# Two b loops of a matmul step become one: which bank each product of a split-precision matmul goes to next

## What is computed

```
h = modulate(rmsnorm(x, g_norm_mix), sh1, sc1);  proj = h @ w_in
y = concat([rg_lru(...) * gelu(gr), pool_mixer(xp)]) @ w_out;  x = x + gt1 * y
h = modulate(rmsnorm(x, g_norm_ffn), sh2, sc2)
x = x + gt2 * ((silu(h @ w_ffn_gate) * (h @ w_ffn_up)) @ w_ffn_down)
...
h = rmsnorm(x, attn_norm_w);  proj = h @ w_in_2            # retention and block attention
x = x + (sigmoid(g_ret) * (o_ret @ w_ret_up) + sigmoid(g_moba) * (o_moba @ w_moba_up)) @ w_out_2
up = causal_dwconv(rmsnorm(x) @ w_ffn_up_2);  x = x + (silu(a) * b) @ w_ffn_down_2
return rmsnorm(x, final_norm_w)
```

## Time and profile before

| | |
|---|---|
| median of three runs | 2616.88 us |
| profiled execution | 2618.59 us |
| its span, first to last instruction | 2616.8 us |
| PE busy | 2538.1 us, 97% |
| PEld busy | 2146.7 us, 82% |
| DVE busy | 1785.6 us, 68% |
| ACT busy | 1180.2 us, 45% |
| mean granted clock of PE | 0.985 |
| DMA | 553.94 MB, 61.3% of 16 engines' span |

### The profile page before, as it was taken

The page is one execution under the profiler, slowest core; times in us unless marked ns, Lnnn a source line. Parts: engine busy times, 40 slices in busy tenths (PEclk is TensorE's granted clock), DMA queues, the critical chain, the costliest instruction groups (busy, mean ns, idle before and its releaser), DMA issues.

```text
span 2616.8 us, 39666 instructions
## 1 busy us (share of the span) xinstructions
PE 2538.1 (97%) x14492; PEld 2146.7 (82%) x14492; DVE 1785.6 (68%) x2301; ACT 1180.2 (45%) x1438; POOL 9.9 (0%) x37
## 2 busy tenths in 40 slices
PE   4999999999999999999999999999999999999997
PEld 0667687888888888888888888888888888888886
DVE  2468698955555555687686565676788668875886
ACT  1345344444444444563444554445544444444443
POOL 1000000000000000000000000000000000000000
PEclk8999998999999999999999999999999999999998
DMA  9968986955555555555554555556555655555553
GB/s 371 403 260 329 382 334 245 357 169 187 191 187 190 186 190 185 164 192 182 178 175 165 166 166 195 183 188 193 177 183 185 202 184 192 190 187 185 185 169 112
DMA packets 156313, 553.94 MB, mean 212 GB/s; under 512 B 16161, under 2 KB 20257, under 8 KB 156209
## 3 DMA queue, kind: packets, MB, share of 16 engines
q1 hardware_dynamic: 155360, 549.85, 61.3%
q0 software_dynamic: 848, 2.69, 0.3%
HBM read 550.38 MB, written 2.10 MB: 211 GB/s over the span
## 4 chain that ended last, share of the span: by engine, by line
PE 89%; DVE 5%; DMA 3%; ACT 1%; issue 1%; SPq 0%; DVEq 0%; ACTq 0%
PE ps L551 54%; PE ps L558 27%; DMA ride<-in_w_ada 3%; PE ps L548 2%; PE pm L579 2%; DVE split L1204 1%; PE ps L555 1%; DVE acc_out L1255 1%; ACT split L872 1%; DVE val L1215 0%; DVE x_t L1327 0%; DVE ssq L1276 0%; PE pm L757 0%; PE pm L662 0%; PE pm L599 0%
## 5 line engine op out<-in xcount | busy, mean ns | idle before, releaser
L1204 DVE TENSOR_TENSOR split<-raw,split 128x1024 fp32r<-128x1024 f32 (+1 forms) x864 | 1031.0, 1203 | 698.9 <-ACT split L872 696.0
L872 ACT ACTIVATE split<-raw 128x1024 fp32r<-128x1024 f32 (+1 forms) x864 | 895.9, 1043 | 1150.6 <-PE ps L558 1095.6
L551 PE MATMUL ps<-h_s,split 128*128 128x512 f32 x3904 | 1242.5, 400 | 13.5 <-DVE split L1204 6.4
L558 PEld LDWEIGHTS ps<-h_s,split 128*128 128x128 f32 x3904 | 738.0, 189 | 175.0
L558 PE MATMUL ps<-h_s,split 128*128 128x256 f32 x3904 | 771.0, 279 | 0.0
L551 PE MATMUL ps<-mid_s,split 128*128 128x512 f32 x2368 | 746.6, 397 | 0.5 <-DVE split L1204 0.4
L551 PEld LDWEIGHTS ps<-h_s,split 128*128 128x128 f32 x3904 | 599.7, 190 | 47.6 <-issue 42.4
L558 PEld LDWEIGHTS ps<-mid_s,split 128*128 128x128 f32 x2368 | 445.5, 188 | 105.5
L558 PE MATMUL ps<-mid_s,split 128*128 128x256 f32 x2368 | 465.7, 278 | 0.0
L551 PEld LDWEIGHTS ps<-mid_s,split 128*128 128x128 f32 x2368 | 361.1, 189 | 7.2 <-issue 5.2
L879 ACT ACTIVATE low<-ps 128x512 f32<-128x512 f32 x232 | 134.4, 579 | 4.4 <-PE ps L558 4.4
(11 more groups left out here) (246 smaller groups left out, 1117.1 us busy)
## 6 DMA issues: line engine op xcount, KB each, us to landing
raw<-in_w_in SPq DMA_DIRECT2D x224, 512.0 KB, 3.3
ride<-in_w_ada SPq DMA_DIRECT2D x64, 1024.0 KB, 8.2
raw<-in_w_ffn_down SPq DMA_DIRECT2D x128, 512.0 KB, 3.5
raw<-in_w_ffn_gate SPq DMA_DIRECT2D x88, 512.0 KB, 3.3
raw<-in_w_ffn_up SPq DMA_DIRECT2D x88, 512.0 KB, 3.5
raw<-in_w_ffn_a SPq DMA_DIRECT2D x88, 512.0 KB, 4.2
raw<-in_w_ffn_b SPq DMA_DIRECT2D x88, 512.0 KB, 4.4
raw<-in_w_out SPq DMA_DIRECT2D x64, 512.0 KB, 5.5
```

The source lines that it names most:

```text
L551: pe.matmul(ps[:, s, b, :], split[:, slot, k, 0, b * P:(b + 1) * P], acts[:, k0 + k, :, :].rearrange("p h t -> p (h t)"), start=start, sto ...
L558: mm = pe.matmul(ps[:, s, b, 0:T], split[:, slot, k, 1, b * P:(b + 1) * P], acts[:, k0 + k, 0, :], start=False, stop=stop)
L872: act.activation(split[:, c, 0:kt, 0, :], raw[:, CHUNKS * s + c, 0:kt, :], ACT.Copy).then_inc(hi_ready, 1)
L1204: dve.tensor_tensor(split[:, c, 0:kt, 1, :], raw[:, CHUNKS * s + c, 0:kt, :], split[:, c, 0:kt, 0, :].bitcast(F32), ALU.subtract).then_inc ...
```

## The change

In each k step the two loops over b are made one. The matmul of 256 columns for a block now stands right behind the one of 512 columns for the same block. The number of matmuls, their operands, waits and increments are the same, and so is the position of the last matmul (b = 1, low weights).

```diff
@@ multiply @@
                 for b in range(2):
                     if tok:
                         pe.matmul(ps[:, s, b, :], acts[:, k0 + k, 0, b * P:(b + 1) * P],
                                   split[:, slot, k, :, :].rearrange("p h n -> p (h n)"), start=start, stop=False)
+                        mm = pe.matmul(ps[:, s, b, 0:SLAB], acts[:, k0 + k, 1, b * P:(b + 1) * P],
+                                       split[:, slot, k, 0, :], start=False, stop=stop)
                     else:
                         pe.matmul(ps[:, s, b, :], split[:, slot, k, 0, b * P:(b + 1) * P],
                                   acts[:, k0 + k, :, :].rearrange("p h t -> p (h t)"), start=start, stop=False)
-                for b in range(2):
-                    if tok:
-                        mm = pe.matmul(ps[:, s, b, 0:SLAB], acts[:, k0 + k, 1, b * P:(b + 1) * P],
-                                       split[:, slot, k, 0, :], start=False, stop=stop)
-                    else:
                         mm = pe.matmul(ps[:, s, b, 0:T], split[:, slot, k, 1, b * P:(b + 1) * P],
                                        acts[:, k0 + k, 0, :], start=False, stop=stop)
             mm.then_inc(chunk_used, 1)
```

## The result

The changed kernel is slower: 2636.67 us is the median of 13 runs, against 2617.17 us for the kernel before (13 runs), a ratio of 1.006 with an interval of 1.0047 to 1.0073. What a median hides is as telling: the runs of before lie within 3 us (2616.65 to 2619.57), those of the changed kernel spread over 19 us (2623.16 to 2642.32). The profiled execution took 2630.16 us. Sixteen more executions of the changed kernel are on record, from 2627.53 to 2642.09 us.

The account below looks back on a forecast made before the run. PE's pace through its k steps was taken to bound the kernel. All terms summed to 0, leaving the profiled 2618.59 us; the runs' median stands 1.7 us lower, so 2616.9 us was forecast, range 2597 to 2651.

Parts of the forecast that it names:

- the price of a same-bank handoff: At the two 512-to-256 handoffs of a step: 5 ns each would give +34 us, 2651 us, the range's upper end.
- The direction that I gave 0.24: The changed kernel comes out slower, because handoffs within one bank cost time; chance 0.24.
- The likeliest case, no change: Whole kernel: no change to within 5.2 us, 2616.9 us with its own range 2611 to 2622; chance 0.56.
- What bounds the kernel, steps and their number: PE's rate through 3392 k steps of 0.696 us sets the time: 2361 us, 90% of the profiled execution.
- Instructions, waits, hand-over points: 0: In each chunk no instruction is added or removed, and waits, increments and hand-over points stay where they were: 0.
- Weight loads: 0 unless they run ahead: Four loads a step, each covered by the matmul ahead: 0; starting two matmuls early would give -54 us, chance 0.08.
- Handoffs: Between a step's matmuls: distance to the next goes with column count, not follower, so 0; rounding allows -54 to +47 us.
- Same bank: 0: A 256 right behind the 512 of its own bank costs nothing extra, judged from the gates' float32 rows: 0.
- The rival on the slower side: Two 512-to-256 handoffs a step cost something within a bank: +34 us at 5 ns, +68 us at 10; chance 0.24.
- Leaving a bank costs: Two of four bank changes a step go: -95 us at 14 ns each, -20 us at 3 ns; chance 0.12.
- The 14 ns a matmul that I asked about: In each 0.696 us step, 0.056 us beyond the columns' time at 2.4 GHz, 14 ns for each of four matmuls.
- A step that differs by more than 1.5 ns proves the forecast wrong: Sign to check in the changed kernel: a step more than 1.5 ns from 0.696 us disproves the forecast, whatever the reason.

Follow-up runs that it names:

- four_wide: Kernel before with every 256-column matmul made 512 wide, so four matmuls of 512 a step: 3318.38 us in one execution.
- six_narrow: Kernel before with every 512-column matmul split into two of 256, each with its own weight load: 2686.95 us in one execution.
- grouped_same_bank: Kernel before with the two 256 of each step in reverse bank order, so two of four handoffs stay in one bank: 2616.71 us, ratio 0.9998.
- starters: Changed kernel with two one-column products put ahead of eleven long stretches: 2620.31 us, 1.0016 of the kernel before.
- alternate_other_bank: Kernel before reordered so 512 and 256 alternate, with about 2 of 16 handoffs within a bank: 2628.67 us, ratio 1.0045.
- alternate_same_bank: Kernel before reordered so 512 and 256 alternate, with 14 of 16 handoffs in one bank: 2629.28 us, ratio 1.0048.
- mixed_two: Kernel before with the changed order only in the feed-forward parts and two one-column products ahead of five long stretches: 2612.86 us, ratio 0.9986.
- mixed_one: Kernel before with the changed order only in the feed-forward parts and one one-column product ahead of five long stretches: 2636.2 us, ratio 1.0075.

## Why the prediction was right and wrong

The range held the time, but by luck more than by reasoning: its upper end was the price of a same-bank handoff, which turned out to cost nothing. The direction that I gave 0.24 was the one that came. The likeliest case, no change, did not come: 2636.67 us is well outside its own 2611 to 2622.

- *What bounds the kernel, steps and their number.* Right. PE's pace is the time; the 3392 steps and the changes per step account for the 11.6 us between the profiled executions to within 0.5 us.
- *Instructions, waits, hand-over points: 0.* Right. PE's waits for others are the same to 0.5 us in each group; ACT's wait for PE grew by 11.5 us, as much as PE fell behind.
- *Weight loads: 0 unless they run ahead.* The forecast says that the same two loads lie under 512 columns; it is the same number but not the same loads (before, those of the second 512 and the first 256; after, those of both 256). All loads have one size, so the term does not change by it. The loads behave as said. At 1030 us in the changed kernel's timeline each still starts with the matmul ahead of it:

```profile
1030.06 0.28 PE L553 MATMUL ps<-h_s,split 128*128 128x256 f32 x1
1030.06 0.19 PEld L551 LDWEIGHTS ps<-h_s,split 128*128 128x128 f32 x1
1030.18 0.39 PE L551 MATMUL ps<-h_s,split 128*128 128x512 f32 x1
1030.18 0.19 PEld L553 LDWEIGHTS ps<-h_s,split 128*128 128x128 f32 x1
```

- *Handoffs: "a matmul's distance to the next goes with its number of columns, not with its follower".* This is the step that failed, in both halves. In equal sizes the distance is the columns' time plus 13.3 ns (four_wide, six_narrow), and in mixed sizes there is a loss that depends on the order over several matmuls: 3.3 ns a step in the order of before, 0 or 13.3 in the changed one (with `o_m` other values). I had argued that two of each size stand in both orders and so the sum stays. A stream's pace is not a sum over its members. The two-to-one of the earlier trace rows that I leaned on was chance: the means of before from 550 to 1100 us, 233.1 and 115.2 ns, are 226.7 + 6.4 and 120 - 4.8, two deviations that happen to meet.
- *Same bank: 0.* Right, and shown (grouped_same_bank). The forecast read one record of the gates' float32 rows as a product; by the starters' rows a product is two records, so 256 columns take 0.43 us and not 0.215, and the row was a still looser bound than said. The rival on the slower side had the right sign, and its lower part the right size, for a reason that is not so.
- *Leaving a bank costs.* Not so: grouped_same_bank leaves a bank half as often as before and takes the same time. alternate_other_bank and alternate_same_bank show the same two paces with 2 and 14 of 16 handoffs in a bank; that their medians are only 0.6 us apart is in part chance, since the runs of the second spread over 18 us. The 14 ns a matmul that I asked about is nearly all the 13.3 ns that equal sizes also have.
- *"A step that differs by more than 1.5 ns proves the forecast wrong."* It did so in both directions, -3.3 ns in some stretches and +10 ns in others, and only the second outweighed the first.

Could it have been foreseen? The size not, since the trace of before has no alternating stream. But its single distances are not constants: a 256 takes 112 to 120 ns and a 512 takes 230 to 236, in a fixed rotation over eight matmuls, without any wait. That was a sign that the pace is a pattern of the whole stream, where a change of order by itself is worth more than the 1.5 ns a step that decide here, and the chance for no change should have been lower. The earlier trace rows had a second sign: the records of `o_m` last 278/281/283 ns where those of the same shape from the other tensors have a median of 277 or 278.

The Trainium skill's page "TensorE: Matmul & The Clock Gate" (Back-to-back issue gap) gives N / 2.4 + 2.5 ns at the full clock as the gap of a matmul without counting a load, and about 131 ns a matmul for pairs of load and matmul of 512 columns. Neither is met by these float32r matmuls with a load each: 512 columns took 226.7 ns, 13.3 over the columns' time, and the least excess of any steady stream of equal sizes was 10.6 ns (256 columns, `o_m`). At the clock of 0.50 the excess is not seen.

What stays open is the cause of the patterns. They do not go with the banks, nor with the other engines' work: mixed_two and mixed_one have the same of it beneath them from 560 to 1120 us, and different patterns. The addresses of the k-tiles within a chunk do not set the period, since the slow one repeats after three pairs where a chunk has eight; but where a tensor starts may matter, as `o_m` suggests, and no run moved a tensor. The slow pattern's 1060 ns are 20 ns over three floor pairs (3 x 346.7), the middle one's 1393.3 ns 6.7 over four. What is shown is that for one and the same tensor the order of sizes decides which patterns exist, that within the long undisturbed stretches a pattern was kept, and that what stands ahead of such a stretch picks it: after two small products fast in 14 of 16 stretches from their start to their end (all five of mixed_two, nine of eleven in starters), after one slow in five of five. Why, and why the stretch from 1546 us went the other way, was not found. Nor was it tested whether the number of products counts or the length of the pause that they make, 0.45 or 0.23 us.

## What to carry to other kernels

When a PE stream has no idle time, compare the distances between starts, record by record, with those of a stream of equal sizes from the same tensor; the difference is the pattern's, and a reordering that changes nothing else can be worth a few tenths of a per cent in either direction. A kernel whose runs spread while another's agree within a few us may have two steady patterns: look at the pace by stretch before explaining the median. Here the grouped order, two 512 and then two 256, gives up 3.3 ns a step for a pace that was the same in all long stretches of every trace, and is the better choice unless the start of each long stretch is controlled.

## What was not expected of the hardware

- A stream of float32r matmuls without waits, at a granted clock of 1.00, can run steadily at 693.3 or at 706.7 ns a step, with the same instructions, over 3449 matmuls on end (the changed kernel) or 3418 (mixed_one).
- In streams of equal sizes a float32r matmul with its load takes 13.3 ns more than its columns at 2.4 GHz, with 256 columns (120.0 ns) as with 512 (226.7 ns).
- With activations from `o_m` the same shapes take 117.3 and 234.4 ns in streams of equal sizes, and of the mixed orders the alternating one is there the faster, 694.1 ns a step against 704.6 grouped.
- One or two one-column products, 0.23 or 0.45 us each time, ahead of five long stretches decided 23 us of the kernel's time.
